# First pair of experts in a two-layer mixture-of-experts trunk: another order on ScalarE and VectorE

## What is computed

```python
for e in range(N_EXPERTS):
    hid = jax.nn.silu(xf @ w_gate_l[e]) * (xf @ w_up_l[e])
    y = y + combine[:, e:e + 1] * (hid @ w_down_l[e])
```

## Time and profile before

| | us |
|---|---|
| median of 3 runs | 999.8 (998.5 to 1000.0) |
| span of the profiled execution | 997.1 |
| time outside that span, against the median | 2.7 |
| PE busy | 948.0 (95%) |
| VectorE (DVE) busy | 826.8 (83%) |
| ScalarE (ACT) busy | 649.3 (65%) |
| GpSimd (POOL) busy | 252.5 (25%) |
| bytes moved | 278.27 MB, mean 279 GB/s |

### The profile page before, as it was taken

How to read it: one execution, slowest core, us unless ns; L and a number is a source line. 1 busy time by engine, 2 the same in 40 slices (tenths; PEclk the granted TensorE clock), 3 DMA queues, 4 the chain that set the end, 5 groups by cost and what they waited for, 6 DMA issues and landing times. The chain is left out here.

```text
span 997.1 us, 15166 instructions
## 1 busy us (share of the span) xinstructions
PE 948.0 (95%) x5086; PEld 783.1 (79%) x5086; DVE 826.8 (83%) x1215; ACT 649.3 (65%) x916; POOL 252.5 (25%) x341
## 2 busy tenths in 40 slices
PE   4999999999999999999969999999999999999994
PEld 4898867678888888888849988787788888888883
DVE  7877667779989989899975676588999899898997
ACT  4345530258888888888744455415888888888882
POOL 1433343361111111110223234435211111111012
PEclk9999999989999999999979999999999999999998
DMA  9853850499999999999894133519999999999966
GB/s 351 290 155 123 259 197 27 179 343 360 365 378 353 369 356 375 362 361 368 223 284 141 58 120 116 219 58 347 390 378 367 370 367 351 368 376 363 360 188 152
DMA packets 118317, 278.27 MB, mean 279 GB/s; under 512 B 8771, under 2 KB 11067, under 8 KB 118238
## 3 DMA queue, kind: packets, MB, share of 16 engines
q1 hardware_dynamic: 99648, 240.40, 67.3%
q0 software_dynamic: 11040, 21.14, 7.4%
q10 hardware_dynamic: 7566, 15.96, 4.5%
HBM read 266.51 MB, written 30.37 MB: 298 GB/s over the span
## 5 line engine op out<-in xcount | busy, mean ns | idle before, releaser
L1542 DVE TENSOR_TENSOR w_lo<-ring,w_hi 128x1024 fp32r<-128x1024 f32 x256 | 301.6, 1228 | 40.0 <-ACT w_hi L2118 37.2
L2118 ACT ACTIVATE w_hi<-ring 128x1024 fp32r<-128x1024 f32 x256 | 260.7, 1058 | 43.5 <-PE PS L1071 27.1
L1023 PE MATMUL PS<-w_hi,x_hi 128*128 128x512 f32 x512 | 164.3, 402 | 2.5 <-ACT w_hi L2118 2.5
L1028 PE MATMUL PS<-w_lo,x_hi 128*128 128x512 f32 x512 | 162.3, 398 | 1.1 <-DVE w_lo L1542 1.1
L1023 PE MATMUL PS<-w_hi,x_lo 128*128 128x512 f32 x512 | 160.8, 395 | 0.7 <-DVE x_lo L1533 0.7
L1549 DVE TENSOR_TENSOR w_lo<-ring,w_hi 128x1024 fp32r<-128x1024 f32 x128 | 154.5, 1220 | 4.3 <-ACT w_hi L2131 4.3
L2131 ACT ACTIVATE w_hi<-ring 128x1024 fp32r<-128x1024 f32 x128 | 135.3, 1059 | 30.6 <-PE PS L1028 28.6
L2460 POOL DMA_INDIRECT M<-xs,idx x30 | 55.2, 1839 | 248.1 <-PE PS L1002 220.9
L1028 PEld LDWEIGHTS PS<-w_lo,x_hi 128*128 128x128 f32 x512 | 96.2, 189 | 25.0 <-DVE w_lo L1542 2.8
L1023 PEld LDWEIGHTS PS<-w_hi,x_lo 128*128 128x128 f32 x512 | 96.6, 189 | 23.9 <-DVE x_lo L1533 1.1
L1023 PEld LDWEIGHTS PS<-w_hi,x_hi 128*128 128x128 f32 x512 | 94.1, 189 | 23.8 <-issue 1.7
(11 more groups left out here) (278 smaller groups left out, 1595.8 us busy)
## 6 DMA issues: line engine op xcount, KB each, us to landing
ring<-in_w_gate SPq DMA_DIRECT2D x32, 2048.0 KB, 15.2
ring<-in_w_down SPq DMA_DIRECT2D x32, 2048.0 KB, 15.8
ring<-in_w_up SPq DMA_DIRECT2D x32, 2048.0 KB
ring<-in_w_in SPq DMA_DIRECT2D x8, 2048.0 KB, 17.7
ring<-in_w_out SPq DMA_DIRECT2D x4, 2048.0 KB, 8.2
ys<-H SPq DMA_DIRECT2D x2, 3072.0 KB, 20.0
H<-ys POOLq DMA_DIRECT2D x12, 512.0 KB, 7.8
M<-in_cache_k ACTq DMA_DIRECT2D x8, 512.0 KB, 4.0
```

Source lines behind the costliest of these rows:

```text
L1023: pe.matmul(PS[:, n, :], x[:, c:c + P], w_hi[j][:, k * 512:(k + 1) * 512], start=(j == 0 and k == 0 and x is x_hi[par]), stop=False)
L1028: mm = pe.matmul(PS[:, n, :], x_hi[par][:, c:c + P], lo[:, k * 512:(k + 1) * 512], start=False, stop=(j == 3 and k == 1))
L1542: dve.tensor_tensor(lo, w, w_hi[j][:, :].bitcast(F32), ALU.subtract).then_inc(up_lo, 1)
L2118: act.activation(w_hi[j][:, :], quarter(3 * par + n, j)[0], ACT.Copy).then_inc(up_hi, 1)
```

## The change

It moves statements in the lists of VectorE (first three hunks) and ScalarE (last three); no operation is added or removed.

- VectorE, pair 0: the rest of expert 1's first gate quarter comes ahead of the rests of its rows (`turned(i, 1)`), and `count_rounds` comes after the last rest of expert 1's up.
- VectorE, prologue: one weight rest instead of two ahead of the first half of expert 0's row rests, and two instead of one behind the second half.
- ScalarE, pair 0: `silu` and the first gate quarter of expert 1 come ahead of the wait for `k_out` and the rounding of expert 1's rows.
- ScalarE: `k_stored`, the issue of the three key stores, comes after the fourth quarter of expert 0's gate instead of ahead of it.

```diff
@@ -1611,10 +1611,9 @@ (vector, pair)
                     if first:
                         split_up(i, 0, 0, range(3, 4))
                         split_up(i, 0, 1, range(4))
+                        split_up(i, 1, 0, range(1))
                         turned(i, 1)
-                        if seated:
-                            count_rounds(l)
-                        split_up(i, 1, 0, range(2))
+                        split_up(i, 1, 0, range(1, 2))
                         gated(i, 0)
                         split_up(i, 1, 0, range(2, 4))
                         split_up(i, 1, 1, range(1))
@@ -1622,6 +1621,8 @@
                         if seated:
                             last_share(l, partial)
                         split_up(i, 1, 1, range(1, 4))
+                        if seated:
+                            count_rounds(l)
@@ -1648,11 +1649,11 @@ (vector, prologue)
                 if seated:
-                    split_up(0, 0, 0, range(2))
+                    split_up(0, 0, 0, range(1))
                     turned_half(0)
                     partial = did(index(rb, 0, key_bank(l) + 1))
                     turned_half(1)
-                    split_up(0, 0, 0, range(2, 3))
+                    split_up(0, 0, 0, range(1, 3))
@@ -2169,13 +2170,16 @@ (scalar, pair)
                     split_up(i, 0, 0, range(3, 4))
+                    if first and seated:
+                        k_stored(l)
                     split_up(i, 0, 1, range(4))
                     if first:
+                        silu(i, 0)
+                        split_up(i, 1, 0, range(1))
                         if seated:
                             act.wait_ge(k_out, 48 * (l + 1))
                         turned(i, 1)
-                        silu(i, 0)
-                        split_up(i, 1, 0, range(4))
+                        split_up(i, 1, 0, range(1, 4))
                         split_up(i, 1, 1, range(1))
@@ -2199,7 +2203,6 @@ (scalar, prologue)
                     split_up(0, 0, 0, range(2, 3))
                     turned_half(0)
                     turned_half(1)
-                    k_stored(l)
```

## The result

The changed kernel has a median of 993.05 us (992.4 to 994.57), beside 999.9 us of the kernel before on the same chip. The ratio is 0.9937, with a 95% interval of 0.9921 to 0.9954. That is faster by 0.6%: 6.3 us by the ratio and at least 4.6, small but clear of the noise (the two medians lie 6.85 us apart). Its own time was 993.13 us, 1.8 above its span, and in every run of the changed kernel and of the experiments the difference is 1.7 to 1.9 us. Ratios use fast runs alone; one run of e7_small_moves, 1064.44 us, was slow and is left out of its ratio.

What follows compares the result with a forecast made beforehand. PE bounds the steady pairs, and its delays sit in the first pair. Gains of 2.3 us in layer 0 and 3.7 in layer 1 make 6.0: span 997.1 to 991.1, plus 2.7 gives 993.8 us, range 992.0 to 997.0.

Steps and rivals of the forecast that it cites:

- the 2.7 us that the sum keeps between span and time: Whole kernel: median 999.8 less profiled span 997.1, added unchanged to the predicted span 991.1.
- Parts 1 and 2: First pair: ScalarE gates and rounds one weight, VectorE rests it, ahead of expert 1's rows; 2.3 us in layer 0.
- Part 3: Start of round: one weight rest before row rests; nothing in layer 0, in layer 1 index and gather 1.0 us earlier.
- Part 2: VectorE, first pair: one weight rest, then row rests, count later; removes 0.85 us of late w_lo in layer 0.
- rival A: Layer 1's gather lands no earlier because key stores leave beside it; gain 3.1 to 5.0, 994.8 to 996.7 us; chance 0.08.
- Part 4: ScalarE issues the three key stores one weight later; cost between nothing and 1.9 us in layer 1, taken as nothing.
- Rival C: Moved stores land as late as weight loads, 17.8 us, and hold expert 1's rows; 1007.8 us; chance 0.05.
- Rival B: Full DMA engines give the time back, layer ends don't move; gain 0 to 2, 998 to 999.8 us; chance 0.06.
- Rival D: PE's slow clock falls in layer 1's ups, 995.8 to 997.3 us, or reverse in layer 0, 990.3 to 991.8; chance 0.07.
- Rival E: A further release late in expert 1 replaces each removed wait; nothing happens, 999.8 us; chance 0.04.
- The sum with the drain: ScalarE's table load charged 1.38 us more: x_hi ends near 218.6, gain some 0.2 us smaller in each layer.
- the signs: Changed profile: PE's w_hi, w_lo, x_lo waits gone; table load near 213.5 and 691, idle time behind the next w_hi.

Runs made afterwards that it cites:

- e7_small_moves: Kernel before with only the key stores issued one weight later and the round count moved behind expert 1's last up rest; ratio 1.0002, 999.80 us.
- e4_silu_first: Kernel before with ScalarE's silu ahead of expert 1's rows, no weight rounded ahead of them, and the round count later; ratio 0.9963, 995.41 us.
- e6_vector_only: Kernel before with only VectorE's order in the first pair changed, ScalarE as before; ratio 1.0053, 1004.60 us.
- e11_scale_late: Kernel before with only GpSimd's scaling moved out of the first pair, behind the scatter of expert 12; ratio 1.0016, 1000.34 us.
- e12: Kernel before with ScalarE's first-pair order changed and GpSimd's scaling moved behind the scatter of expert 12; ratio 0.9990, 998.23 us.
- e3_prologue_only: Kernel before with only VectorE's start of the round changed, one weight rest instead of two ahead of the row rests; ratio 1.0006, 999.12 us.
- e8_stores_late: Changed kernel with the key stores issued behind the fourth quarter of expert 0's up; ratio to the kernel before 1.0065, 1006.64 us.
- e9: Changed kernel with the key stores issued behind the first quarter of expert 0's up; ratio to the kernel before 0.9947, 993.64 us.
- e10: Changed kernel with the key stores issued behind the second quarter of expert 0's up; ratio to the kernel before 0.9948, 993.57 us.
- e2_pair_only: Kernel before with only the first pair's order changed on ScalarE and VectorE, start of the round and stores as before; ratio 0.9942, 992.99 us.

## Why the prediction was right, and where it was not

**The whole.** 993.8 was forecast, from 6.0 us less in the two first pairs; measured is 993.05, with 2.47 and 3.76 us less on the stretches named. The likeliest case is the one that happened. How nearly the numbers meet is partly luck. The stretch of layer 1 was 3.76 us shorter in this trace and 3.25 in the second one, against 3.7 in the sum. And the 2.7 us that the sum keeps between span and time is no such term: a run's time lies 1.8 us above its own span, so the 2.7 held 0.9 of scatter between the profiled execution of the kernel before and its median. With 1.8 the sum gives 992.9, with 2.7 it gives 993.8, and 993.05 lies between. What the runs show as due to the change is 2.48 (C0), 2.85 (C1) and 0.3 (the gather's earlier landing), 5.6 us of the 6.0; the rest of the 6.23 is luck: the routing's slow stretch held PE up ahead of the ups of layer 1, where the gather covered it.

**Parts 1 and 2.** Right in mechanism and size, but for the prices told below. The table load stands at 212.36 and 689.41; ScalarE's idle time took both silu and the first w_hi. In layer 0 the sum gave 2.3, and C0 fell by 2.48. For layer 1 it left 2.7 once Part 3's 1.0 is taken off, and C1 fell by 2.85. The split into "silu ahead" and "weight ahead" that the sum didn't make comes from e4_silu_first, and e6_vector_only shows that VectorE's half has a sign of its own.

**The price of a weight rest**, which the sum took at 1.2 us for each, is where Part 2 is incomplete. It put the 0.85 us of late w_lo in layer 0 down to the round count and the order. The count cost nothing: VectorE stood idle behind it for 0.92 us, as the earlier trace rows say, and e7_small_moves, with the count moved, has a C0 of 10.39 against 10.38. With the scaling moved away (e11_scale_late) C0 is 0.66 us shorter, which is most of the 0.85. The row it cited had the answer in it: two rests at 220.06 took 3.20 us, more than two times 1.2. In the changed kernel the three behind the gating product, in ns, shortest, median and longest, are

```profile
L1542 DVE TENSOR_TENSOR w_lo<-ring,w_hi x3: 1465/2051/2053, 219.3 to 222.6; 128x1024 fp32r<-128x1024 f32 x3
```

and they still cost PE nothing, since the new order left them in front of their need. e12 shows the cause. The Trainium skill, page "SBUF — State Buffer", section "Who interferes with whom", says that a VectorE instruction with two inputs in SBUF contends with a GpSimd instruction that reads SBUF, and that the pair of ports which the two engines share is an exclusive lock. The trace agrees: a rest goes from 1.21 to 2.05 us and a scaling from 1.04 to 2.01, while the gating product of 128x512, which has one input in PSUM, keeps its 0.68 us in the middle of the scaling (218.67, the scaling runs from 217.53 to 225.60). Had the sum used it, Part 2's margins behind the gating product would have been seen to be thinner, with the same total.

**Part 3** was mis-sized. The 1.0 us rests on the step "the gather starts from the index, 1.0 us earlier, and landed at about 694.0, so now 693.0". The 0.70 us at x_lo did go, and w_lo 1 with its margin of 0.1 us held. But what followed was 0.3 us: the index did come 1.1 us earlier and the gather took 0.8 us longer. e3_prologue_only alone has D1 0.35 us shorter and no gain that can be measured. This is the half of rival A that did happen, with 0.7 of its 1.0 us. The reason that it gave, the key stores that now leave beside the gather, is not borne out: e3 has them in their old place and lands at the same 25.1 us. What sets the landing, as far as the traces tell, is all that stands ahead of it in the DMA engines: the weight loads, and in both orders the stores, which cost it 1.4 to 2 us. In the changed kernel's own trace D1 is 0.91 us shorter, close to the forecast of 1.0, by the luck of the slow stretch.

**Part 4** cost nothing, as taken, and the bound was sound. Rival C's mechanism exists, but not where the change puts the stores. e8_stores_late brings it about by issuing them four quarters later still. That its 1006.64 us is near the rival's 1007.8 is chance: the stores took 11.2 us, and not 17.8. The rival put the point from which it decides at a landing of 14 us, from 204.6. In the runs it is the place of issue: as long as the stores leave before the weight load of about 210 they land in time. What the rival left out is the clock: after the 7.95 us PE came back at 0.50.

**Rival B**, the gain given back, is refuted by the ends that moved rigidly by 3.6 us in layer 0. **Rival D** is a mechanism that exists: slow stretches moved the first two quarters by 0.87 us, the projection by 0.6 and the routing by 1.1, in both directions, the last by where the stretch fell and not by its length. The Trainium skill, page "TensorE: Matmul & The Clock Gate", section "Part 1: The HAM clock gate (the "warmup" mystery)", says that the end of a slow stretch varies between runs of one kernel; the two traces of the changed kernel agree, at 0.62 and 0.50 from 204 to 208. But it is noise on both sides and not the gain, since C0 and C1 are the same within 0.02 us in four traces of three kernels. **Rival E** fell with the waits of PE.

**The table load.** It took 1.28 us and began 0.02 us after the rounding, as in the earlier trace rows, and silu began 0.02 us after its end (212.36 + 1.28 = 213.64, silu at 213.66). The sum with the drain had x_hi end near 218.6, which is 217.4 on this trace with its lead of 1.16 us (208.29 against 209.45); it ended at 216.1. (That sum is also too small in its own terms: it sets the row rests against a need at 219.6, where Part 2 has them needed at 219.2.) Of the signs, the idle time behind the next w_hi didn't come in layer 0, where x_hi followed at once, and was 0.23 us in layer 1; no wait of PE hangs on it.

**The best version** measured is the changed kernel. e9, e10 and e2_pair_only, which leaves out Parts 3 and 4, don't differ from it by more than the measurement tells.

## What to carry to other kernels

Idle time of the engine that feeds the bottleneck is worth most when work that doesn't depend on the awaited input is moved into it; then look at the engine behind, because its order has to follow (by medians ScalarE's alone gave 1.8 us, VectorE's alone lost 5.1, both gave 5.6). Divide the duration of every group by its count before using a "typical" price: 3.20 us for two is a contention that a price of 1.2 hides. A transfer that lands late beside full DMA engines may gain little from an earlier start: 1.1 us earlier gave 0.3 here, and stores moved from ahead of it to behind it gave 1.4 to 2.

## What the runs showed of the hardware

- A VectorE subtraction of 128x1024 with both inputs in SBUF takes 1.21 us alone and 2.05 beside GpSimd's scaling of 128x1024, which itself goes from 1.04 to 2.01. Moving the scaling moves the loss.
- Stores of 0.8 MB behind two weight loads of 2 MB landed 11.2 us after the last issue; issued just ahead of them, about 6.6 us after it. In layer 1 of the first of these kernels they landed 8.7 us after the first issue.
- A gather landed 25.0 to 25.8 us after the first of three loads ahead of it was issued, whether its index came 16.0 or 17.05 us after that issue, and 23.3 and 23.9 us after it when 0.8 MB of stores stood behind the gather and not ahead.
- The same slow stretch of the clock (0.89 and 0.90 in the mean of the routing) cost PE 1.1 us more where it fell behind a wait for VectorE than where it fell ahead of it.
- After 7.95 us of idle time PE's products took 1.22 and 1.05 us instead of 0.63 for some 6 us (granted clock 0.50 to 0.57), so that waiting 8 us cost 11.3. The 1.32 and 2.50 us of e6_vector_only were followed by products at half clock too (0.50 from 223.5 to 226).
